# Dilated attention of four heads in another order: the first group in natural order with a softmax of its own, values by pairs of heads, and two waits of the FFN moved

## The reference

```python
ATT_PATTERNS = ((128, 1), (512, 4), (2048, 16))   # window, dilation; 3 groups x 4 heads of 128
h = rmsnorm(x, norm_w) * (1.0 + scale) + shift     # shift, scale, gate = c_act @ w_ada + b_ada
qa, ka, va, za, ... = split(h @ w_in)
for g, (window, dil) in enumerate(ATT_PATTERNS):   # key t - j*dil, j = 0..window//dil, causal
    o, lse = dilated_window_attention(qa[:, :, g], ka[:, :, g], va[:, :, g], window, dil)
wts = softmax(stack(lses), axis=0)
o_att = sum(wts[..., None] * stack(outs))          # one softmax over the keys of all three groups
y_att = o_att.reshape(B, S, ATT_OUT) * silu(za)
merged = sigmoid(ga) * (y_att @ w_proj_attn) + sigmoid(gr) * (y_ret @ w_proj_ret)
```

## Time and profile before

| | |
|---|---|
| median of 3 runs | 2731.32 us (2729.35 to 2734.41) |
| profiled execution, its own time | 2728.5 us |
| its span | 2726.8 us |
| mean granted TensorE clock | 0.983 |
| TensorE matmul busy | 2643.9 us, 97% |
| VectorE, ScalarE, GpSimd busy | 45%, 35%, 15% |
| DMA moved | 269.39 MB, mean 99 GB/s |

### The profile page before, as it was taken

One profiled execution on the slowest core, in us unless ns is written; L12 is line 12 of the kernel. 1 busy time (PEld: TensorE's weight loads), 2 busy tenths in 40 slices (PEclk: granted clock), 3 DMA queues, 4 the chain that ended last, 5 costly groups with the idle time before them and its releaser, 6 DMA issues.

```text
span 2726.8 us, 33510 instructions
## 1 busy us (share of the span) xinstructions
PE 2643.9 (97%) x13229; PEld 2217.8 (81%) x13245; DVE 1213.8 (45%) x1645; ACT 965.2 (35%) x1289; POOL 410.3 (15%) x428
## 2 busy tenths in 40 slices
PE   7999999999999999998999999999999999999998
PEld 7887778777888878786888888888888888888887
DVE  5435554744534765634433333443443333343435
ACT  6425454225324412213433332323253333322222
POOL 3104332200000100000301001321021001032300
PEclk9989999999999999999999999999999999999999
DMA  5210003222242554522222223122222222322122
GB/s 202 92 62 17 17 17 105 92 82 78 93 178 85 186 185 151 188 78 93 93 95 100 90 100 113 68 104 77 94 84 101 92 92 98 124 83 94 72 102 76
DMA packets 43592, 269.39 MB, mean 99 GB/s; under 512 B 5128, under 2 KB 5264, under 8 KB 16224
## 3 DMA queue, kind: packets, MB, share of 16 engines
q1 hardware_dynamic: 32080, 227.59, 23.3%
q0 software_dynamic: 11120, 39.27, 4.2%
q10 hardware_dynamic: 288, 1.05, 0.1%
HBM read 265.79 MB, written 2.10 MB: 98 GB/s over the span
## 4 chain that ended last, share of the span: by engine, by line
PE 65%; issue 23%; DVE 6%; POOL 4%; ACT 2%; DMA 1%; DVEq 0%; POOLq 0%; SPq 0%; ACTq 0%
PE PS L1888 63%; DVE w_split L1148 1%; POOL merged L586 1%; PE PS L2113 1%; POOL res_lo L580 1%; POOL res_hi L580 1%; ACT w_split L623 1%; POOL merged L525 1%; DMA raw<-in_weights 1%; DVE small L1446 1%; DVE R L1534 0%; DVE h_act L1156 0%; DVE ks_lo L1383 0%; PE PS L2335 0%; PE PS L1975 0%
## 5 line engine op out<-in xcount | busy, mean ns | idle before, releaser
L1888 PE MATMUL PS<-h_act,w_split 128*128 128x512 f32 (+1 forms) x5856 | 1271.2, 379 | 12.7 <-DVE w_split L1148 3.8
L1888 PEld LDWEIGHTS PS<-h_act,w_split 128*128 128x128 f32 x5856 | 1054.2, 190 | 215.0 <-issue 4.3
L1148 DVE TENSOR_TENSOR w_split<-raw,w_split 128x2048 fp32r<-128x2048 f32 x213 | 504.6, 2369 | 905.0 <-ACT w_split L623 888.2
L623 ACT ACTIVATE w_split<-raw 128x2048 fp32r<-128x2048 f32 x213 | 407.7, 1914 | 824.4 <-PE PS L1888 815.7
L1888 PE MATMUL PS<-w_split,h_act 128*128 128x512 f32 (+1 forms) x1728 | 410.8, 387 | 4.5 <-DVE w_split L1148 3.3
L1888 PEld LDWEIGHTS PS<-w_split,h_act 128*128 128x128 f32 x1728 | 314.1, 190 | 60.2 <-DVE w_split L1148 4.3
L1888 PE MATMUL PS<-y_act,w_split 128*128 128x512 f32 x1152 | 265.4, 391 | 2.2 <-DVE w_split L1148 2.2
L1888 PEld LDWEIGHTS PS<-y_act,w_split 128*128 128x128 f32 x1152 | 217.5, 189 | 47.8 <-DVE w_split L1148 2.6
L1888 PE MATMUL PS<-R 128*128 128x128 f32 (+3 forms) x896 | 190.3, 364 | 9.7 <-ACT R L1041 5.5
L1888 PEld LDWEIGHTS PS<-R 128*128 128x128 f32 x896 | 135.2, 201 | 42.6 <-issue 15.5
L1888 PE MATMUL PS<-w_split,res_hi 128*128 128x384 f32 x512 | 130.9, 336 | 0.0
(11 more groups left out here) (276 smaller groups left out, 2144.9 us busy)
## 6 DMA issues: line engine op xcount, KB each, us to landing
raw<-in_weights SPq DMA_DIRECT2D x213, 1024.0 KB, 4.8
R<-in_w_ada POOLq DMA_DIRECT2D x36, 512.0 KB, 5.0
gate_bc<-in_w_ada POOLq DMA_DIRECT2D x12, 512.0 KB, 4.9
R<-in_nsa_wk POOLq DMA_DIRECT2D x1, 2048.0 KB, 10.3
xres<-in_x POOLq DMA_DIRECT2D x1, 2048.0 KB, 10.8
R<-in_decay POOLq DMA_DIRECT2D x8, 256.0 KB, 3.3
out<-R SPq DMA_DIRECT2D x3, 512.0 KB, 2.6
xres<-in_x ACTq DMA_DIRECT2D x2, 512.0 KB, 4.0
```

The lines of the kernel that those rows point to most:

```text
L623: act.activation(w_split[:, 0, half, :, :], raw[:, half, :, :], ACT.Copy).then_inc(w_hi, 1)
L1148: dve.tensor_tensor(w_split[:, 1, half, :, :], raw[:, half, :, :], w_split[:, 0, half, :, :].bitcast(F32), ALU.subtract).then_inc(w_lo, 1)
L1888: return pe.matmul(out, lhsT, rhs, start=start, stop=stop, skip_group_check=True)
```

## The change

Per layer, the four v groups become three of full width: `v0`, the values of g = 0 for all four heads with rows in natural order, and `pair0` and `pair1`, the values of g = 1 and 2 for two heads each, by residue. Their panels are put together by DMA from the old ones in pieces of 512 and 1024 bytes.

Queries and keys of g = 0 keep their natural order, so a block of 128 queries needs only its own and the previous block of keys: seven blocks of 128 by 128 instead of sixteen. g = 0 then has its own softmax (maximum and sum for four query blocks), g = 1 and 2 have one for four residue classes. To join them, each side needs the other's maximum and sum in its own order: VectorE spreads the 16 numbers of a partition (`spread`), two matmuls of 32 columns against constant 0/1 matrices move them between partitions (`swap`), VectorE picks (`chosen`, `others`), ScalarE exponentiates the difference, and both sides scale their probabilities by 1 / (own sum + weight x other sum). The values of both sides are added in one PSUM bank; those by residue are written with a stride of four elements.

The heads are written out and overlapped by one: transposes and values of head h - 1 stand behind k of head h; `swap(h - 1)` stands behind the 31st matmul of q of head h (of the gate group for the last head). The 8 modulation matmuls move from behind za into the first retention group. In the FFN the first down group waits for `y_act` by halves, and the 24 one-column matmuls stand one by one behind every second matmul of the next up group. The same halves are used in the last down group and in the first projection of `merge_att`. VectorE's FFN loops are written out too, its first `ada_panel` of the second chunk stands behind the read of the columns.

```diff
+HEAD_SETS = (Sets(0, 1, 1, 0, 1, 7), Sets(0, 1, 0, 1, 0, 3), Sets(1, 0, 0, 1, 0, 3), Sets(1, 0, 1, 1, 1, 4))
+PAIR_SETS = (0, 1)
...
+        P0_block = [P0[:, 768:896]] + [P0[:, 256 * k:256 * k + 256] for k in range(TB - 1)]
...
+        PTa = [M1[:, 2048:2560], M1[:, 2560:3072], M1[:, 3072:3584], R0[:, 3072:3584]]
+        v_natural = [R2[:, k * W:(k + 1) * W] for k in (0, 1, 2, 7)]
...
+            def load_values(g, panel, heads, lo, width):
...
                 for half in range(2):
                     sp.wait_ge(w_lo, 2 * g + half - 1)
...
+                    for h in range(heads):
+                        sp.dma_start(raw[:, half, :, h * width:(h + 1) * width],
+                                     weights[panel + h, half, :, :].rearrange("p (k n) -> p k n", k=4)[:, :, lo:lo + width]
+                                     ).then_inc(raw_in[half] if h == heads - 1 else raw_pieces[half], 16)
...
                 with pool.Fori(0, AH) as h:
-                    it = AH * l + h
-                    for r in range(RES):
-                        pool.wait_ge(a_fac, RES * it + r + 1)
-                        pool.tensor_tensor(Pa[r], Pa[r], fac[:, r:r + 1].to_broadcast([P, 768]),
-                                           ALU.mult).then_inc(a_p, 1)
+                    pool.wait_ge(a_fac, AH * l + h + 1)
+                    for probs, share in ((P0_block[0].unsqueeze(1), shares_of[:, 0, 0:1]),
+                                         (P0[:, 0:768].rearrange("p (q k) -> p q k", q=TB - 1), shares_of[:, 0, 1:TB]),
+                                         (P12, shares_of[:, 1, :])):
+                        pool.tensor_tensor(probs, probs, share.unsqueeze(2).to_broadcast(list(probs.shape)), ALU.mult
+                                           ).then_inc(a_p, 1)
...
+                def exps(h):
+                    it, bank = AH * l + h, 4 * HEAD_SETS[h].s
+                    act.wait_ge(a_mx, 2 * it + 1)
+                    for r in range(RES):
+                        last = act.activation(P12[:, r, :], PS[:, bank + r // 2, r % 2 * 256:r % 2 * 256 + 256], ACT.Exp,
+                                              bias=stats[:, 1, 0, r:r + 1], accum_out=stats[:, 1, 1, r:r + 1])
+                    last.then_inc(a_exp, 1)
+                    act.wait_ge(a_mx, 2 * it + 2)
+                    for qb in range(TB):
+                        lo, width = (qb - 1) % TB * 256, 256 if qb else P
+                        last = act.activation(P0_block[qb], PS[:, bank + 2 + lo // W, lo % W:lo % W + width], ACT.Exp,
+                                              bias=stats[:, 0, 0, qb:qb + 1], accum_out=stats[:, 0, 1, qb:qb + 1])
+                    last.then_inc(a_exp, 1)
+                    act.wait_ge(a_apart, it + 1)
+                    act.activation(weight, apart, ACT.Exp).then_inc(a_weight, 1)
...
+                    dve.wait_ge(a_s, 2 * it + 1)
...
+                    dve.reduce_max(stats[:, 0, 0, 1:TB], banded[:, 0:768].rearrange("p (q k) -> p q k", k=256), AX, negate=True)
+                    dve.reduce_max(stats[:, 0, 0, 0:1], banded[:, 768:896], AX, negate=True).then_inc(a_mx, 1)
+                    dve.wait_ge(a_mx, 2 * it + 2)
+                    dve.wait_ge(a_exp, 2 * it + 2)
+                    dve.tensor_tensor(spread, stats.rearrange("p s k a -> p s (k a)").unsqueeze(3).to_broadcast([P, 2, 8, 4]),
+                                      pick.unsqueeze(2).to_broadcast([P, 2, 8, 4]), ALU.mult).then_inc(a_spread, 1)
+                    dve.wait_ge(a_swap, it + 1)
...
+                    att.link(dve.tensor_tensor(shares_of, weight, others[:, :, 1, :], ALU.mult))
+                    att.link(dve.tensor_tensor(shares_of, shares_of, stats[:, :, 1, :], ALU.add))
+                    dve.reciprocal(shares_of, shares_of).then_inc(a_fac, 1)
...
+            def group_with_columns(c, ch):
+                for n, _ in enumerate(dense(c, 0, H)):
+                    col = n // 2 - 4
+                    if n % 2 == 0 or not 0 <= col < ADA_COLS:
+                        continue
+                    if col == 0:
+                        pe.wait_ge(set_free[1], at("ffn.ada", ch).u1)
+                        pe.wait_ge(ada_summed, ch + 1)
+                    ins = mm(PS[:, 4, col:col + 1], ada_acc[:, col // 4, col % 4 * P:(col % 4 + 1) * P],
...
+                    elif i == 0:
+                        group_with_columns(at("ffn.up.a", ch, i), ch - 1)
...
-                pe.wait_ge(act_lo, c.l)
-                for n in range(2):
-                    group(c.plus(C(g=n)), n, Yr, feat=False)
...
-                pe.wait_ge(set_free[0], at("ffn.ada", ch).u0)
-                pe.wait_ge(ada_summed, ch + 1)
-                for col in range(ADA_COLS):
-                    last = mm(PS[:, 0, col:col + 1], ada_acc[:, col // 4, col % 4 * P:(col % 4 + 1) * P],
-                              cf[:, C_ONE:C_ONE + 1], True, True)
...
+                group(c, 0, Yr, feat=False, lows=(c.l - 4, c.l))
+                group(c.plus(C(g=1)), 1, Yr, feat=False)
+            group_with_columns(at("ffn_up0"), 1)
...
-            group(c, 1, Yr, feat=False, kph=(4, 2))
+            group(c, 1, Yr, feat=False, kph=(4, 2), lows=(c.l - 2, c.l))
...
+                def scores(h):
...
+                    pe.wait_ge(qk_ready, 2 * NG * (it + 1))
+                    for r in range(RES):
+                        bank, lo = 4 * S + r // 2, r % 2 * 256
+                        mm(PS[:, bank, lo:lo + 256], ident_b, cb[:, B_D2:B_D2 + 256], r % 2 == 0, False)
...
-                            last = mm(PS[:, b0 + 1, (g - 1) * P:g * P], qa[:, g, r * P:(r + 1) * P],
+                            last = mm(PS[:, bank, lo + (g - 1) * P:lo + g * P], qa[:, g, r * P:(r + 1) * P],
                                       ka[:, g, r * P:(r + 1) * P], False, True)
...
+                    for qb in (1, 2, 3, 0):
+                        bank, lo = 4 * S + 2 + (qb - 1) % TB // 2, (qb - 1) % 2 * 256
+                        if qb:
+                            mm(PS[:, bank, lo:lo + P], causal, ident_b, lo == 0, False)
+                            lo += P
+                        mm(PS[:, bank, lo:lo + P], ident_b, causal, False, False)
+                        first = max(qb - 1, 0) * P
+                        lo = (qb - 1) % 2 * 256
+                        last = mm(PS[:, bank, lo:lo + (qb + 1) * P - first], qa[:, 0, qb * P:(qb + 1) * P],
+                                  ka[:, 0, first:(qb + 1) * P], False, True)
+                    last.then_inc(a_s, 1)
...
+                    bank = 4 * HEAD_SETS[h].s
+                    pe.wait_ge(a_spread, AH * l + h + 1)
+                    mm(PS[:, bank, 0:32], to_natural, spread[:, 1].rearrange("p a b -> p (a b)"), True, True)
+                    mm(PS[:, bank, 32:64], to_residue, spread[:, 0].rearrange("p a b -> p (a b)"), False, True
+                       ).then_inc(a_swap, 1)
...
+                    for n, (kb, qb) in enumerate(natural):
+                        if n % 4 == 0:
+                            pe.wait_ge(*((a_ptd, 2 * it + 1) if n else (a_pta, 2 * it + 1)))
+                        mm(out[:, qb * P:(qb + 1) * P], v_natural[kb][:, mine], PTa[n // 4][:, n % 4 * P:(n % 4 + 1) * P], n == 0, False)
...
+                        if r % 2 == 0:
...
+                            lo = (h % 2 * 2 + g) * P
+                            slot = r % 2 * 2 + g
+                            last = mm(out.rearrange("p (i r) -> p r i", r=RES)[:, r, :], v_residue[r][:, lo:lo + P],
+                                      PTa[2 + r // 2][:, slot * P:(slot + 1) * P], False, True)
...
+                group(at("layer.v0", l), 1, Hr, feat=False)
+                group(at("layer.q0", l), HEAD_SETS[0].q, H, n=NG)
+                group(at("layer.k0", l), HEAD_SETS[0].k, H, n=NG)
+                pe.wait_ge(residues_ready, 2 * KT * (l + 1))
+                group(at("layer.pair0", l), PAIR_SETS[0], residues, feat=False)
+                scores(0)
+                for h in range(1, AH):
+                    group(at(f"layer.q{h}", l), HEAD_SETS[h].q, H, n=NG, behind={30: lambda: swap(h - 1)})
+                    group(at(f"layer.k{h}", l), HEAD_SETS[h].k, H, n=NG)
+                    transposes(h - 1)
+                    values(h - 1)
+                    if h == 2:
+                        group(at("layer.pair1", l), PAIR_SETS[1], residues, feat=False)
+                    scores(h)
...
+                group(at("layer.merge_att.gate", l, 0), 0, H, behind={30: lambda: swap(AH - 1), 71: last_head})
...
+                group(c, 1, Y, kph=(2, 2), lows=(c.l - 2, c.l))
...
+                group(at("layer.ret.qk", l, 0), 0, H, between=modulation)
```

More of the change, by code:

```diff
@@ L1331, in _ @@
             line = own = Chain(dve, own_start)
[L1332 removed]
+            line.put(dve.memset(spare, 1.0))
             def two_rows(two):
@@ L1764, in _, with keys @@
-                    dve.sem_inc(y_ready, 1)
-                    own.end()
```

(39 more changed lines are left out.)

388 lines of the change are left out of this document (229 added, 159 removed).

## The result

| | before | after |
|---|---|---|
| median | 2730.34 us (4 runs, 2726.47 to 2734.41) | 2640.49 us (4 runs, 2637.24 to 2642.69) |
| profiled execution, span | 2728.5 us, 2726.8 us | 2639.4 us, 2637.7 us |
| mean granted clock | 0.983 | 0.991 |

The ratio is 0.967, 95% interval 0.9652 to 0.9688: 90 us faster. The forecast was 2639 us, with a range of 2630 to 2657.

A forecast was written before the change was run, and what follows sets the result against it. TensorE, busy 97% of the span, was taken as the bound. Heads -74.4, FFN waits -6.5 and columns -10.6 sum to -91.5 us on the profiled 2728.5, giving 2637, or 2639 for a median; range 2630 to 2657.

The forecast's parts named there:

- Less work in the heads: TensorE per head: dense values -0.36 us, scores -2.39, nine fewer transposes -1.02, nine fewer values -2.01, swap of statistics +0.44.
- GpSimd's wait: Attention heads: TensorE's wait for GpSimd's scaled probabilities goes, as they are due two dense groups later; -2.09 us a head.
- The gap ahead of the scores: Attention heads: scores' wait for ScalarE's last copy of k goes, with transposes and values now between; -0.84 us a head.
- Clock in the heads: Two attention stretches: without GpSimd's wait TensorE's clock no longer falls; -8.2 us in all.
- Strided writes: Eight value matmuls a head writing PSUM at stride four: taken as 0; rival at half pace +14.3 us, 2653, chance 0.16.
- FFN waits: FFN down groups: starting on the first four k-tiles removes three waits for `y_act`; -6.5 us.
- columns: FFN up groups: 48 one-column matmuls among wide ones cost 0.218 us each, two bare weight loads, without clock loss; -10.6 us.
- The rival that the clock falls in the interleaved group too: FFN up group with columns: clock falls there too, or loads pile up, columns no cheaper; +10.6 us, 2650, chance 0.12.
- Statistics late: Attention heads: `swap` is due 7.1 us behind the scores; a chain 3 us longer makes TensorE wait; +13 us, 2652, chance 0.13.
- The slower case: Attention heads: clock falls in each 9.2 us block of small instructions; 95 us, 2734 on the median, chance 0.02.

The follow-up runs named there:

- swap_early: The changed kernel with the swap of the statistics behind the 11th matmul of the group and not the 31st: 2674.26 us, ratio 0.9800.
- scaling_short_before: The kernel before with GpSimd scaling 8 columns of each block of probabilities and not 768: 2730.80 us, ratio 1.0004.

## Why the prediction was right, and where it was not

- **Less work in the heads: right.** Per head, forecast and measured: dense values -0.36 and -0.42, scores 4.15 and 4.28, fifteen transposes 1.70 and 1.65, fifteen values 3.35 and 3.42, swap 0.44 and 0.36. The scores' 0.13 lie in the three blocks of g = 0 with 256 columns (0.60 each with its masks, where columns alone give 0.56) and in the 3% taken off; whether the short masks cause it isn't shown. The period came out at 58.95 and not 58.7 also because q and k took 32.9 with the swap between them, where 144 x 0.2276 are 32.8, and because the pieces reckoned for the head before sum to 67.06 us where 66.95 were measured. Times eight that is the 2 us by which the heads fell short.
- **"GpSimd's wait", -2.09 a head: size right, cause wrong.** The step that was wrong is the one that took the releaser from the wait list and built the cover on "the scaled probabilities are now due later". With GpSimd's work cut away the kernel before did not get faster; with one copy moved ahead of one exponential it got 15.6 us faster. The wait went away in the changed kernel all the same. The reason is read from the code and not tested by a run of its own: the fifteen transposes of a head now go into four PSUM banks and wait for no copy, where six of one residue had to wait until the banks of the last six were copied out. And the copies, which the values still wait for, no longer stand behind exponentials of the same head. The prediction had the copies pass beside the transposes "as they nearly do now", while one of them was the wait it wanted to explain. That the number came out in spite of this is luck. Had the change only made GpSimd's part cheaper, the same reasoning would have forecast some 11 us that do not exist.
- **The gap ahead of the scores, -0.84: right**; nothing stands idle there.
- **Clock in the heads, -8.2: right.** Period times eight gives -64.0, the clock -8.2, together -72.2 of the -72.4 measured. The exchange in the kernel before gives 8.2 for the same thing in its trace, and 7.0 by the medians.
- **Strided writes, 0: right.** Four matmuls take 0.89 us with the stride and without it. The Trainium skill (PSUM — Partial Sum Buffer, Specifications (TRN2)) has any non-contiguous access slow matmuls significantly; for 128-column float32 matmuls at a stride of four elements this case measures no cost, and the measurement decides.
- **FFN waits, -6.5, and columns, -10.6: right.** The stretch gave -16.9 of -17.1. Put back one at a time they cost 8.3 and 6.6 by the medians, together 14.9, and 8.3 and 7.5 in the traces, together 15.8; the burst of that run has none of the 0.44 us waits for its result that stood behind it before, and it lost less clock than the two bursts of before. A column costs 0.233 us, 0.015 more than the two loads at the burst's pace. The Trainium skill (TensorE: Matmul & The Clock Gate, Step-by-step: what each phase is for) lets weight loads be pulled ahead of running matmuls. Were all hidden, 44 columns would have cost almost nothing; they cost 10.5 us. The rival that the clock falls in the interleaved group too did not come: it was 1.00 there.
- **Rivals.** Statistics late: the margin was 1.1 us, so the mechanism was near, and its price, by `swap_early`, is 34 us for a swap due 20 matmuls (4.5 us) earlier, which made TensorE wait 2.6 to 3.3 us in each head. GpSimd's scaling took 5.7 us and not 3.7 in six heads, but 17.7 us were in hand there, and 3.5 in the last head. The slower case was far: a block of 12.7 us of small whole matmuls kept clock 1.00.

## What to carry to other kernels

In this profile a wait's releaser was the engine that finished last, by 0.1 us, and not the one that the time hung on; before building on it, list what the waiting instruction's semaphores need, and look at every engine whose work ends within a few tenths of a microsecond. Each engine works off its list in order, so what stands ahead of a cheap copy can make it late: here 0.6 us of copy behind two exponentials cost 16 us in the program, and an exchange of two lines gave it back. Price a wait of 2 us or more near small matmuls above its own length, since the clock may fall behind it. Spread one-column matmuls among wide ones instead of running them in a burst.

## What the runs showed of the hardware

- **Length of a wait and the clock.** In the attention heads it fell behind five of eight waits of 2.0 us, and in `scaling_short_before` behind five of eight again, not all the same ones. It fell behind six of eight waits of 2.6 to 3.3 us, behind two of two of 4.2, and behind none of sixteen of 0.9 (two runs, their profiled executions). In the kernel before five falls cost 8.2 us, 1.6 each; in `swap_early` six cost at most 12.9 us, 2.2 each. In the FFN, where a wait of 2.0 to 2.2 us stands between groups of wide matmuls, it fell behind one of fifteen (five runs with three such waits).
- **What is executed matters too, not only waiting.** 48 records of one column, without a wait, dropped the clock within 2.2 and 4.8 us; 60 records of 128 columns behind 15 transposes, 12.7 us with the scores, did not.
- **GpSimd and VectorE side by side.** The same GpSimd instruction takes twice as long in six of the eight heads. By form, in the changed kernel, head 0 and head 3:

```profile
L647 POOL TENSOR_TENSOR merged<-merged,cm 128x1024 f32<-128x1024 f32 x1 | 3.9, 3940 | 0.0
...
L647 POOL TENSOR_TENSOR merged<-merged,cm 128x1024 f32<-128x1024 f32 x1 | 1.9, 1893 | 0.0
```

Both are longer where they overlap; that the one holds up the other is read from this overlap, and no run separates it. VectorE's low half of the weights lies over the first and not over the second (it starts at 1549.75, when GpSimd is done). In the first case GpSimd ends at 1402.00, 1.75 us behind VectorE's end at 1400.25, which is nearly the whole 1.89 of the undisturbed instruction, as if it had waited for VectorE. VectorE's instruction took 2.82 against 2.29 us:

```profile
1397.43 2.82 DVE L1252 TENSOR_TENSOR w_split<-raw,w_split 128x2048 fp32r<-128x2048 f32 x1 [1.23 <-ACT w_split L684]
...
1549.75 2.29 DVE L1252 TENSOR_TENSOR w_split<-raw,w_split 128x2048 fp32r<-128x2048 f32 x1 [3.98 <-ACT w_split L684]
```

My 3.7 us for the scaling was therefore 5.7 in those heads. It cost nothing, with 17.7 us of cover (1419.73 - 1402.0); in the last head 3.5 us were left.
